# Filter taps in two transfers, two row tiles scaled on GpSimd, the third row tile split, and the first product ahead of the fifth tile

## The chip, the cores and the metric

The kernel runs on one core of a Trainium2 chip. The metric is the device time of one execution in microseconds. Three runs of the kernel before took 942.45, 942.81 and 944.39 us; their median is 942.81.

## The reference

It is one inference step of a two-layer decoder over a prompt of 512 rows and 64 sample rows (8 sequences of 8), each of 1024 features. Layer one is a Conformer convolution layer: h = rms_norm(x) and a, b, z = h @ w_in with w_in of 1024 x 3072. Then a * sigmoid(b) goes through a 31-tap depthwise convolution, and layer norm, silu gates, an output product and a residual follow. Layer two is sparse attention with three branches (compressed, selected, window) over keys and values projected once. What the change touches is the beginning:

```
def rms_norm(x, g):
    xf = x.astype(jnp.float32)
    y = xf * lax.rsqrt(jnp.mean(xf * xf, axis=-1, keepdims=True) + EPS)
    return (y * g.astype(jnp.float32)).astype(x.dtype)
...
    h = rms_norm(x, g_pre)
    a, b, z = jnp.split(h @ w_in, 3, axis=-1)
```

## The kernel before, in words

The 576 rows are five row tiles: four of 128 prompt rows and one (t=4) of the 64 sample rows. Each engine runs one instruction stream in the order written; streams meet only at semaphores. Queues are fed by the engine that issues a transfer: SP (row tiles, weights, state), ScalarE (taps and vectors), GpSimd (page table).

The start works as follows. SP loads the row tiles into `x_first` (L518 to L520), then waits for the third (L559, L560) before it issues weight chunks 0 and 1, two transfers of convolution state after chunk 1 (L563 to L565), and chunks 2 to 5. A weight chunk is a 1024 x 128 piece of w_in (512 KB). Chunk 6 and later ones wait for a slot of a ring of six. ScalarE issues the taps (31 rows into `vec_rows`, L780), six vectors of one row each (L781 to L783), and four small tables.

Per row tile ScalarE squares and sums (L806), VectorE makes the mean (L1272), ScalarE the root (L794), VectorE the reciprocal (L1290, L1292). The scaled tile goes to `xn_a`, which has two slots: VectorE scales tiles 0 to 2 (`first_scale`, L1295), ScalarE tiles 3 and 4 (L811). TensorE transposes a scaled tile in eight 128-column pieces (L1834) into one of two pairs of PSUM banks. VectorE multiplies that by the norm's gain into `h_whole` (`first_turn`, L1300). The gain comes from `vec_rows`, transposed by TensorE after tile 1 (L1839) and copied by VectorE (L1309).

Each product is done as three: a value is split in a high part (fp32r, copied by ScalarE: `first_hi`, `split_hi_a`, both through the copy helper at L777) and a low part (value minus high part: `first_lo` on VectorE, L1284; `split_lo_a` for weights and the low part of tile 3 on GpSimd, L674 and L680). TensorE adds hi x hi, hi x lo and lo x hi.

```
            def first_half(c, hf):
                for k in range(KD):
                    out, here = pb((2, 0)[c] + hf, HT), slice(hf * HT, hf * HT + HT)
                    pe.matmul(out, tile_hi[:, c, k], h_hi[:, k, here], start=(k == 0), stop=False)
                    pe.matmul(out, tile_hi[:, c, k], h_lo[:, k, here], start=False, stop=False)
                    ins = pe.matmul(out, tile_lo[:, c, k], h_hi[:, k, here], start=False, stop=(k == KD - 1))
```

The first two chunks are multiplied in halves of 288 rows: `first_half(0, 0)`, `first_half(1, 0)`, then (0, 1) and (1, 1), each 24 matmuls. The first half needs the tiles 0 and 1 and 32 columns of tile 2, but waits for the low parts of three whole tiles. Chunks 2 to 23 follow as whole products (L1801 to L1803); three chunks feed each of eight convolution blocks on VectorE, ScalarE and GpSimd. `small_tables` on TensorE makes a bias table (L1820) and turns two small rows (L1823), ahead of the transposes of tile 4.

## Time and profile before

| | |
|---|---|
| median of three runs | 942.81 us |
| profiled execution, its own time | 943.98 us |
| its span | 942.2 us |
| TensorE matmul busy | 896.2 us (95%) |
| VectorE, ScalarE, GpSimd busy | 539.6, 439.3, 307.1 us |
| chain that ended last: TensorE's share | 88% |
| granted TensorE clock, mean | 0.989 |

The page gives busy time by engine and the chain of work that ended last. A share of busy time is a mean over stages with different limits, so the start must be read by itself. PE is TensorE, PEld its weight load, DVE VectorE, ACT ScalarE, POOL GpSimd, SP the engine that issues most transfers; a q behind a name is that engine's sequencer issuing a transfer.

### The profile page before, as it was taken

The numbers are of one execution on the slowest core, as the hardware profiler recorded it, in microseconds if no ns is written. First come the engines' busy times: TensorE is split into PE (matmuls) and PEld (weight loads), VectorE is DVE, ScalarE is ACT, GpSimd is POOL, SyncE is SP. The second block draws the span as 40 slices with busy tenths as digits, with TensorE's granted clock in tenths as the row PEclk, the third lists the DMA queues.
The fourth block names the chain that finished last, engine by engine and source line by source line (L and its number), as shares of the span: only waits on it lengthen the run. The fifth ranks groups of instructions, "written<-read, shape, count | busy, mean of one in ns | idle before, by whom it ended". The sixth has DMA issues, their size and how long they took to land.

```text
span 942.2 us, 16720 instructions
## 1 busy us (share of the span) xinstructions
PE 896.2 (95%) x6250; PEld 764.3 (81%) x6250; DVE 539.6 (57%) x1183; ACT 439.3 (47%) x897; POOL 307.1 (33%) x313
## 2 busy tenths in 40 slices
PE   3899999998999999999999999999999999899995
PEld 2799999954478877778989998989999998786653
DVE  2478999998863573331244554555564555544563
ACT  4567677633512533232454555545554555423421
POOL 1479988863370000003014232323233233300000
PEclk9999999998999999999999999999999999999997
DMA  7455433129049443166322231322223002913521
GB/s 205 106 126 167 122 104 88 57 52 304 17 155 371 186 149 90 33 146 181 82 58 49 65 87 29 89 46 68 50 65 67 24 2 53 278 69 109 158 80 35
DMA packets 158137, 99.53 MB, mean 106 GB/s; under 512 B 97173, under 2 KB 146997, under 8 KB 157976
## 3 DMA queue, kind: packets, MB, share of 16 engines
q1 hardware_dynamic: 143198, 79.16, 31.6%
q0 software_dynamic: 4896, 10.32, 3.0%
q10 hardware_dynamic: 9961, 8.97, 2.9%
q8 instruction: 51, 0.84, 0.4%
q14 instruction: 31, 0.25, 0.1%
HBM read 89.58 MB, written 18.85 MB: 115 GB/s over the span
## 4 chain that ended last, share of the span: by engine, by line
PE 88%; ACT 4%; DVE 3%; issue 2%; DMA 1%; POOL 0%; SPq 0%; DVEq 0%; ACTq 0%; POOLq 0%
PE psum L1782 10%; PE psum L2113 7%; PE psum L1881 6%; PE psum L1801 6%; PE psum L1802 6%; PE psum L1803 6%; PE psum L2114 6%; PE psum L2115 6%; PE psum L2208 6%; PE psum L2178 4%; PE psum L2143 4%; PE psum L2161 3%; PE psum L2029 3%; PE psum L2028 3%; PE psum L2030 3%; ACT arena L1188 2%
## 5 line engine op out<-in xcount | busy, mean ns | idle before, releaser
L2113 PE MATMUL psum<-u_hi,tile_hi 128*128 128x288 f32 x464 | 145.9, 314 | 3.3 <-ACT arena L777 3.0
L777 ACT ACTIVATE arena<-psum 128x512 f32<-128x512 f32 (+9 forms) x214 | 82.3, 433 | 142.5 <-PE psum L2030 48.8
L756 POOL TENSOR_SCALAR arena<-arena,kept 128x512 f32<-128x512 f32 (+3 forms) x128 | 83.5, 667 | 174.3 <-DVE kept L1648 174.3
L2114 PE MATMUL psum<-u_lo,tile_hi 128*128 128x288 f32 x464 | 137.4, 296 | 0.0
L2115 PE MATMUL psum<-u_hi,tile_lo 128*128 128x288 f32 x464 | 136.6, 294 | 0.0
L1346 DVE SCALAR_TENSOR_TENSOR psum<-arena,psum 128x512 f32<-128x512 f32 x168 | 127.0, 756 | 6.0
L1801 PE MATMUL psum<-h_hi,tile_hi 128*128 128x288 f32 x352 | 104.2, 296 | 0.0
L1802 PE MATMUL psum<-h_lo,tile_hi 128*128 128x288 f32 x352 | 103.8, 295 | 0.0
L1803 PE MATMUL psum<-h_hi,tile_lo 128*128 128x288 f32 x352 | 103.8, 295 | 0.0
L2113 PEld LDWEIGHTS psum<-u_hi,tile_hi 128*128 128x128 f32 x464 | 87.1, 188 | 14.7 <-issue 6.5
L1579 DVE COPY arena<-psum 128x512 f32<-128x512 f32 (+3 forms) x72 | 37.0, 513 | 101.6 <-PE psum L2161 99.0
L1188 ACT ACTIVATE arena<-arena,kept 128x512 f32<-128x512 f32 (+3 forms) x128 | 70.6, 554 | 44.4 <-DVE kept L1614 44.4
L2114 PEld LDWEIGHTS psum<-u_lo,tile_hi 128*128 128x128 f32 x464 | 87.3, 188 | 1.7 <-issue 1.7
L2115 PEld LDWEIGHTS psum<-u_hi,tile_lo 128*128 128x128 f32 x464 | 87.1, 188 | 0.0
L1782 PE MATMUL psum<-arena 128*128 128x256 f32 (+2 forms) x448 | 84.7, 350 | 0.0
L1782 PEld LDWEIGHTS psum<-arena 128*128 128x128 f32 (+1 forms) x448 | 71.5, 183 | 11.5 <-issue 0.2
L674 POOL TENSOR_TENSOR tile_lo<-tile_whole,tile_hi 128x1024 fp32r<-128x1024 f32 x24 | 59.0, 2464 | 44.8 <-ACT tile_hi L777 44.8
L1802 PEld LDWEIGHTS psum<-h_lo,tile_hi 128*128 128x128 f32 x352 | 66.9, 190 | 0.0
L1801 PEld LDWEIGHTS psum<-h_hi,tile_hi 128*128 128x128 f32 x352 | 66.3, 188 | 0.0
L1803 PEld LDWEIGHTS psum<-h_hi,tile_lo 128*128 128x128 f32 x352 | 66.2, 188 | 0.0
L777 ACT ACTIVATE tile_hi<-tile_whole 128x1024 fp32r<-128x1024 f32 x56 | 59.1, 1056 | 6.7 <-PE psum L1803 5.5
L2208 PE MATMUL psum<-arena 128*128 128x256 f32 x256 | 59.0, 380 | 1.3 <-POOL arena L763 1.3
(295 smaller groups left out, 1835.7 us busy)
## 6 DMA issues: line engine op xcount, KB each, us to landing
tile_whole<-in_b_w_in SPq DMA_DIRECT2D x64, 256.0 KB
tile_whole<-in_a_w_in SPq DMA_DIRECT2D x24, 512.0 KB
arena<-in_cmp_w SPq DMA_DIRECT2D x4, 2048.0 KB, 10.0
kvw_whole<-in_w_kv SPq DMA_DIRECT2D x6, 1024.0 KB, 11.4
bias_copies<-bias_line POOLq DMA_DIRECT2D x4, 1280.0 KB, 23.2
arena<-in_x_prompt SPq DMA_DIRECT2D x8, 512.0 KB, 8.9
arena<-in_a_w_out SPq DMA_DIRECT2D x4, 1024.0 KB, 11.4
arena<-bias_copies SPq DMA_DIRECT2D x16, 256.0 KB, 3.7
```

Of the source, the lines that this page charges most:

```text
L756: pool.tensor_scalar(L, L, rden[:, stat(n) + k:stat(n) + k + 1], gR[:, i, h:h + 1], ALU.mult, ALU.mult).then_inc(S["pn_ready"], 1)
L777: return nc.scalar.activation(out, in_, ACT.Copy, scale=scale)
L1188: nc.scalar.activation(L, L, ACT.Exp, scale=-1.0, bias=mn[:, k:k + 1], accum_out=den[:, k:k + 1]).then_inc(S["exp_done"], 1)
L1346: V.scalar_tensor_tensor(out=acc_p, in0=glu_p[:, m, w:w + SEQ], scalar=tap, in1=acc_p, op0=ALU.mult, op1=ALU.add).then_inc(S["conv_step"], 1)
L1782: ins = pe.matmul(out, l, r, start=(k == 0), stop=(k == len(pairs) - 1))
L1801: pe.matmul(out, w_hi[:, k], h, start=(k == 0), stop=False)
L1802: pe.matmul(out, w_hi[:, k], l, start=False, stop=False)
L1803: ins = pe.matmul(out, w_lo[:, k], h, start=False, stop=(k == KD - 1))
L2113: pe.matmul(pb(7, HT), w_hi, u_hi[:, k, here], start=(k == 0), stop=False)
L2114: pe.matmul(pb(7, HT), w_hi, u_lo[:, k, here], start=False, stop=False)
L2115: ins = pe.matmul(pb(7, HT), w_lo, u_hi[:, k, here], start=False, stop=(k == KD - 1))
L2208: ins = pe.matmul(pb(4 + 2 * (t % 2), 4, CH)[:, c], yT[:, k, t * P:(t + 1) * P], chunk_sb(C_OB + c)[:, k], start=(k == 0), stop=(k == KD - 1))
```

## The change

The taps (31 rows) are loaded by two transfers of 16 and 15 rows. `xn_a` has a place for each tile (tiles 0 and 2 share one, tiles 1 and 4 another). GpSimd scales tiles 3 and 4 (`first_scale_far`) in place of ScalarE. The third tile's turned columns are treated in two parts, 32 and 96 columns, so that there are six row groups (`ROW_GROUPS`) in place of five for `first_turn`, `first_hi` and `first_lo`; the counts of the waits follow. SP no longer waits for the third row tile before the weights. ScalarE does the square of tile 4 after the first three high parts, and the split of weights 0 ahead of the first high part. TensorE transposes the taps after tile 0, and runs `first_half(0, 0)` before the small tables and the transposes of tile 4.

```diff
@@ -136,7 +136,7 @@
...
         last_rows_in = at(R_X + 2 * D, 4, KV, P)
-        xn_a = at(R_C, 2, D)
+        xn_a = [at(R_C, D), at(R_C + D, D), at(R_C, D), at(R_Z + 2560, D), at(R_C + D, D)]
         state_rows = at(R_C + 2 * D, 2, D)
@@ -450,6 +450,8 @@
...
+        ROW_GROUPS = [slice(0, P), slice(P, 2 * P), slice(2 * P, HT), slice(HT, 3 * P), slice(3 * P, 4 * P), slice(4 * P, NT)]
         def square_slot(m):
@@ -556,8 +558,6 @@
...
                     sp.wait_ge(S[name], count)
-                if c == 0:
-                    sp.wait_ge(x_in[2], 16)
                 for src, how in parts:
@@ -674,9 +674,18 @@
...
+            def first_scale_far(t):
+                r = rows(t)
+                pool.wait_ge(S["rs_a"], t - 2)
+                if t == 4:
+                    pool.wait_ge(S["tr_a"], 2)
+                pool.tensor_scalar(xn_a[t][0:r], x_first[0:r, t], rs[0:r, t:t + 1], None, ALU.mult).then_inc(S["xn_a_ready"], 1)
+            first_scale_far(3)
             split_lo_a(0)
+            first_scale_far(4)
             split_lo_a(1)
-            pool.wait_ge(S["hh_ready"], 4)
+            pool.wait_ge(S["hh_ready"], 5)
             pool.tensor_tensor(out=h_lo[:, :, 3 * P:4 * P], in0=h_whole[:, :, 3 * P:4 * P], in1=h_hi[:, :, 3 * P:4 * P],
@@ -777,7 +786,8 @@
...
-            act.dma_start(vec_rows[0:W], I["a_conv_w"][0]).then_inc(S["vec_in"], 16)
+            for lo, hi in ((0, 16), (16, W)):
+                act.dma_start(vec_rows[lo:hi], I["a_conv_w"][0, lo:hi]).then_inc(S["vec_in"], 16)
             for n, name in enumerate(("a_norm_pre", "a_conv_b", "a_ln_g", "a_ln_b", "kv_norm", "b_norm_pre")):
@@ -793,22 +803,21 @@
...
-            def first_hi(t):
-                act.wait_ge(S["h_ready"], t + 1)
-                here = slice(t * P, t * P + rows(t))
+            def first_hi(g):
+                act.wait_ge(S["h_ready"], g + 1)
+                here = ROW_GROUPS[g]
                 copy(h_hi[:, :, here], h_whole[:, :, here]).then_inc(S["hh_ready"], 1)
...
-            for t in range(TT):
+            def first_square(t):
                 r = rows(t)
...
                 first_root(t)
-                if t >= 3:
-                    act.wait_ge(S["rs_a"], t - 2)
-                    act.wait_ge(S["tr_a"], t - 1)
-                    nc.scalar.activation(xn_a[0:r, t % 2], x_first[0:r, t], ACT.Copy, scale=rs[0:r, t:t + 1]).then_inc(S["xn_a_ready"], 1)
+            for t in range(4):
+                first_square(t)
@@ -816,17 +825,19 @@
...
+            split_hi_a(0)
             first_hi(0)
-            split_hi_a(0)
             first_hi(1)
             first_hi(2)
+            first_square(4)
             split_hi_a(1)
+            first_hi(3)
+            first_hi(4)
             act.wait_ge(S["early_mm"], 1)
...
             copy(pe_sb, pb(1, 2, 16)).then_inc(S["line_part"], 1)
-            first_hi(3)
-            first_hi(4)
+            first_hi(5)
             split_hi_a(2)
@@ -1278,9 +1289,9 @@
...
-            def first_lo(t):
-                dve.wait_ge(S["hh_ready"], t + 1)
-                here = slice(t * P, t * P + rows(t))
+            def first_lo(g):
+                dve.wait_ge(S["hh_ready"], g + 1)
+                here = ROW_GROUPS[g]
                 V.tensor_tensor(out=h_lo[:, :, here], in0=h_whole[:, :, here], in1=h_hi[:, :, here], op=ALU.subtract).then_inc(S["hl_ready"], 1)
@@ -1292,12 +1303,14 @@
...
                     dve.wait_ge(S["tr_a"], t - 1)
-                V.tensor_scalar(xn_a[0:r, t % 2], x_first[0:r, t], rs[0:r, t:t + 1], None, ALU.mult).then_inc(S["xn_a_ready"], 1)
-            def first_turn(t):
-                r = rows(t)
+                V.tensor_scalar(xn_a[t][0:r], x_first[0:r, t], rs[0:r, t:t + 1], None, ALU.mult).then_inc(S["xn_a_ready"], 1)
+            def first_turn(g):
+                here = ROW_GROUPS[g]
+                t = here.start // P
+                lo, hi = here.start - t * P, here.stop - t * P
                 dve.wait_ge(S["tr_a"], t + 1)
-                V.tensor_tensor(out=h_whole[:, :, t * P:t * P + r], in0=pb(4 + 2 * (t % 2), KD, P)[:, :, 0:r], in1=gain(0, r),
+                V.tensor_tensor(out=h_whole[:, :, here], in0=pb(4 + 2 * (t % 2), KD, P)[:, :, lo:hi], in1=gain(0, hi - lo),
                                 op=ALU.mult).then_inc(S["h_ready"], 1)
@@ -1307,8 +1320,6 @@
...
             V.tensor_copy(vecT, pb(2, KD, 37)).then_inc(S["vec_ready"], 1)
-            first_mean(4)
-            first_scale(4)
             dve.wait_ge(S["vec_ready"], 1)
@@ -1316,9 +1327,13 @@
...
             first_lo(2)
+            first_mean(4)
+            first_scale(4)
             first_turn(3)
             first_turn(4)
-            first_lo(4)
+            first_lo(3)
+            first_turn(5)
+            first_lo(5)
@@ -1422,7 +1437,7 @@
...
             def kv_rows_lo(t):
-                dve.wait_ge(S["hh_ready"], TT + t + 1)
+                dve.wait_ge(S["hh_ready"], TT + 1 + t + 1)
                 here = slice(t * P, t * P + rows(t))
@@ -1823,21 +1838,22 @@
...
-            for t in range(TT):
+            def turn_a(t):
                 r = rows(t)
-                if t == TT - 1:
-                    small_tables()
                 pe.wait_ge(S["xn_a_ready"], t + 1)
                 if t >= 2:
-                    pe.wait_ge(S["h_ready"], t - 1)
+                    pe.wait_ge(S["h_ready"], (1, 2, 4)[t - 2])
                 for k in range(KD):
-                    ins = pe.transpose(pb(4 + 2 * (t % 2), KD, P)[:, k, 0:r], xn_a[0:r, t % 2, k * P:(k + 1) * P], ident[0:r, 0:r])
+                    ins = pe.transpose(pb(4 + 2 * (t % 2), KD, P)[:, k, 0:r], xn_a[t][0:r, k * P:(k + 1) * P], ident[0:r, 0:r])
                 ins.then_inc(S["tr_a"], 1)
-                if t == 1:
-                    pe.wait_ge(S["vec_in"], 16 * 7)
-                    for k in range(KD):
-                        ins = pe.transpose(pb(2, KD, 37)[:, k], vec_rows[0:37, k * P:(k + 1) * P], ident[0:37, 0:37])
-                    ins.then_inc(S["vec_ps"], 1)
+            turn_a(0)
+            pe.wait_ge(S["vec_in"], 16 * 8)
+            for k in range(KD):
+                ins = pe.transpose(pb(2, KD, 37)[:, k], vec_rows[0:37, k * P:(k + 1) * P], ident[0:37, 0:37])
+            ins.then_inc(S["vec_ps"], 1)
+            for t in range(1, 4):
+                turn_a(t)
@@ -1895,12 +1911,14 @@
...
             first_half(0, 0)
+            small_tables()
+            turn_a(4)
             pe.wait_ge(S["line_part"], 3)
...
             first_half(1, 0)
-            pe.wait_ge(S["hl_ready"], 4)
+            pe.wait_ge(S["hl_ready"], 5)
             pe.wait_ge(S["lo_pool"], 3)
-            pe.wait_ge(S["h_ready"], TT)
+            pe.wait_ge(S["h_ready"], TT + 1)
             for m in range(KD):
@@ -2042,7 +2060,7 @@
...
                 if n < 5:
-                    pe.wait_ge(S["hl_ready"], TT - 1 + (2, 2, 4, 4, 5)[n])
+                    pe.wait_ge(S["hl_ready"], TT + (2, 2, 4, 4, 5)[n])
                 r = rows(t)
```

## Rows read from the trace of the kernel before

**Rows 1.** The page, the chain that ended last, share of the span by engine.
```profile
PE 88%; ACT 4%; DVE 3%; issue 2%; DMA 1%; POOL 0%; SPq 0%; DVEq 0%; ACTq 0%; POOLq 0%
```

**Rows 2.** Stretches: length, busy PE PEld DVE ACT POOL (count), clock, DMA, GB/s.
```profile
0.00:10.00 10.00, 0.49 (x3) 0.53 (x4) 1.07 (x3) 2.84 (x5) 2.48 (x14) 1.00 0.77 243
50.00:100.00 50.00, 50.00 (x381) 50.00 (x381) 42.45 (x62) 32.00 (x41) 42.49 (x28) 1.00 0.55 150
220.00:240.00 20.00, 15.86 (x49) 8.52 (x49) 16.28 (x21) 10.71 (x17) 5.85 (x3) 0.74 0.65 216
```

**Rows 3.** The chain in order of time, 0 to 80 us: start, length, what.
```profile
2.16 13.26 DMA arena<-in_x_prompt
```

**Rows 4.** Single microseconds of the start; the last two columns are DMA share, GB/s.
```profile
7.00:8.00 1.00, 0.00 (x0) 0.00 (x0) 0.02 (x1) 0.95 (x2) 0.00 (x0) 1.00 1.07 362
11.00:12.00 1.00, 0.45 (x3) 0.04 (x1) 0.10 (x1) 0.87 (x2) 0.00 (x0) 1.00 0.06 25
16.00:17.00 1.00, 0.56 (x6) 0.57 (x6) 0.15 (x1) 0.78 (x3) 0.00 (x0) 1.00 1.11 319
```

**Rows 5.** Timeline of ScalarE: start, length, line, out<-in, count, idle before and releaser.
```profile
6.80 1.06 ACT L806 ACTIVATE arena<-arena 128x1024 f32<-128x1024 f32 x1 [2.10 <-DMA arena<-in_x_prompt]
...
8.17 0.20 ACT L794 ACTIVATE kept<-kept 128x1 f32<-128x1 f32 x1 [0.22 <-DVE kept L1272]
10.72 1.06 ACT L806 ACTIVATE arena<-arena 128x1024 f32<-128x1024 f32 x1 [2.35 <-DMA arena<-in_x_prompt]
...
13.39 1.06 ACT L806 ACTIVATE arena<-arena 128x1024 f32<-128x1024 f32 x1 [1.10 <-DMA arena<-in_x_prompt]
...
15.44 1.06 ACT L806 ACTIVATE arena<-arena 128x1024 f32<-128x1024 f32 x1 [0.48 <-DMA arena<-in_x_prompt]
...
25.37 1.04 ACT L777 ACTIVATE tile_hi<-tile_whole 128x1024 fp32r<-128x1024 f32 x1
...
29.80 0.57 ACT L777 ACTIVATE arena<-psum 16x512 f32<-16x512 f32 x1
```

**Rows 6.** Timeline of VectorE.
```profile
8.61 0.75 DVE L1295 TENSOR_SCALAR arena<-arena,kept 128x1024 f32<-128x1024 f32 x1
...
19.96 2.36 DVE L1300 TENSOR_TENSOR h_whole<-psum,arena 128x1024 f32<-128x1024 f32 x2
25.50 1.23 DVE L1284 TENSOR_TENSOR h_lo<-h_whole,h_hi 128x1024 fp32r<-128x1024 f32 x1 [3.18 <-ACT h_hi L777]
...
27.77 3.39 DVE L1284 TENSOR_TENSOR h_lo<-h_whole,h_hi 128x1024 fp32r<-128x1024 f32 x2
```

**Rows 7.** Timeline of TensorE.
```profile
9.51 1.94 PE L1834 MATMUL psum<-kept,arena 128*128 128x128 f32 x8 [9.51 <-DVE arena L1295]
...
16.43 1.07 PE L1839 MATMUL psum<-kept,arena 37*128 37x37 f32 x8 [1.13 <-DMA arena<-in_b_norm_pre]
...
24.91 1.89 PE L1820 MATMUL psum<-arena 32*16 32x512 f32 x2
26.73 0.39 PE L1823 MATMUL psum<-kept,arena 16*128 16x16 f32 x2
28.00 1.09 PE L1834 MATMUL psum<-kept,arena 64*128 64x64 f32 x8 [0.89 <-DVE h_whole L1300]
31.27 0.58 PE L1889 MATMUL psum<-h_hi,tile_hi 128*128 128x288 f32 x1 [2.17 <-DVE h_lo L1284]
...
36.66 0.29 PE L1890 MATMUL psum<-h_lo,tile_hi 128*128 128x288 f32 x1
```

**Rows 8.** GpSimd: its timeline, then one of its groups by shape (count | busy, mean ns).
```profile
26.50 2.45 POOL L674 TENSOR_TENSOR tile_lo<-tile_whole,tile_hi 128x1024 fp32r<-128x1024 f32 x1 [22.98 <-ACT tile_hi L777]
29.97 3.44 POOL L674 TENSOR_TENSOR tile_lo<-tile_whole,tile_hi 128x1024 fp32r<-128x1024 f32 x1 [1.03 <-ACT tile_hi L777]
...
L756 POOL TENSOR_SCALAR arena<-arena,kept 128x512 f32<-128x512 f32 x32 | 24.4, 774 | 102.1 <-DVE kept L1648 102.1
```

**Rows 9.** Timeline of SP's queue.
```profile
0.75 1.83 SPq L520 DMA_DIRECT2D arena<-in_x_prompt  x4
```

## The prediction

> **What bounds the kernel now.** I read three views in this order. The page's chain that ended last is 88% TensorE by share of the span [rows 1]. The table of stretches shows TensorE busy 50.00 of 50.00 us in a projection stretch, and only 15.86 of 20.00 us around 220 to 240 us, at a granted clock of 0.74 [rows 2]. The reader should see that once the projections run TensorE has no holes, so nearly every microsecond by which its stream starts earlier is a microsecond off the end. The chain in order of time then shows what the start waits for: 13.26 us of the prompt's fourth row tile (t=3) in flight, before its normalisation can begin [rows 3]. The first dense product starts at 31.27 [rows 7]. The case is therefore the first 31 us.
>
> **Why the rows come so late.** The table by microsecond [rows 4] shows the DMA engines at share 1.07 and 362 GB/s in 7 to 8 us, but at 0.06 and 25 GB/s in 11 to 12 us. A share of 0.06 is 1/16: one engine works alone. In the first 10 us 243 GB/s moved 2.4 MB, about the five row tiles (2.3 MB): the rest of the wait is for one engine's share. One transfer of this stretch has a row count that sixteen engines can't share evenly: the taps, 31 rows of 4 KB, 124 KB. On one engine at 25 GB/s they take 124/25 = 5.0 us, which is the length of the tail (10 to 15 us). The squares of the four prompt tiles start at 6.80, 10.72, 13.39 and 15.44 [rows 5]: 2 to 4 us apart, where 512 KB at 362 GB/s is 1.4 us. SP issues all row tiles from 0.75 us on [rows 9], and its next issue waits for the third tile, so the weights' bytes only show at 16 to 17 us (319 GB/s) [rows 4].
>
> **The change part by part.**
>
> *Taps in two transfers (16 and 15 rows).* If they spread over 16 and 15 engines, the busiest engine carries 8 KB of taps in place of 124. The tiles then follow each other at 1.4 us. With the first at 6.1 us (6.80, less the 0.7 by which halved sharing with the taps may bring it forward; bounds 5.4 and 6.8), they land at about 6.1, 7.5, 8.9 and 10.3, the fifth at 11. Bounds: if both parts stay on one engine, the arrivals are those of now. If only the 15 rows do, they cost 60/25 = 2.4 us. I take the even spread. The vectors' seven rows are seen by TensorE at 16.43 now, last behind that same engine [rows 7]. They should be there by 8, and are first needed at 10.7.
> The Trainium skill, "DMA: Bandwidth & Descriptors", section "Why a DMA increments its semaphore by 16 and not by 1", says that a transfer uses the largest number of engines up to 16 that divides its slowest dimension: 1 engine for 31 rows, 15 for 15 rows. The trace agrees for the first. For the second no row here shows it.
>
> *SP's wait on the third tile gone.* Chunks 0 and 1, the state rows and chunks 2 to 5 queue straight behind the row tiles. All eight transfers move forward, about 4 MB. If the queue serves in order, chunk 0 (512 KB at 319 GB/s = 1.6 us from about 10, and 1 to 1.5 us until it is seen, an estimate from the tail, whose 5.0 us end at 15 while the last vector is seen at 16.43) is there at 12.5 to 13.2 instead of after 16. Cost to the tiles: nothing if in order, up to the whole backlog if not (second-last rival).
>
> *ScalarE.* One tile takes 6.80 to 8.37 (square, VectorE's mean, root ending 8.17 + 0.20) [rows 5], 1.6 us. Four in a row from 6.1 start at 6.1, 7.7, 9.3, 10.9: now the engine sets the pace, not the DMA. VectorE's reciprocal of the fourth ends about 1.8 us after its square starts, 12.7. The fifth tile's square and both scalings (copies at L811) leave this stretch. The copy of weights 0 (1.04) [rows 5] runs at 13.2 to 14.3 and then the first h_hi at 14.5 to 15.6.
>
> *GpSimd's two scalings.* No row shows a 128x1024 scaling there. The nearest is 0.77 us for 128x512 [rows 8]; below, 0.75 us as VectorE's [rows 6], above twice 0.77 = 1.55. I take 1.2. The fourth tile is scaled by 13.9, needed at 16.5; the fifth by 21.3, needed at 26. Both are hidden, with 2.6 us and 4.7 us of cover; the first one holds the split of weights 0 back by 1.2 us at most.
>
> *TensorE.* Row tile 0: 8.8 to 10.8 (as at 9.51, 1.94 us). Taps: to 11.8 (1.07). [rows 7] Row tile 1: to 13.8. VectorE's copy of the taps follows its fourth reciprocal, 12.7 to 13.2, then the turns 0 and 1 (2.36 for both [rows 6]): 13.25 to 14.4 and to 15.6. Row tile 2 waits for turn 0: 14.6 to 16.5; row tile 3: to 18.5.
>
> *VectorE up to the first product.* Here two-input work of VectorE meets GpSimd's. Alone, a low part takes 1.23 us; the pair at 27.77 takes 3.39 instead of 2.4 [rows 6], beside the split of weights 0 that ends at 28.95 (26.50 + 2.45), and the split after it takes 3.44 instead of 2.45 [rows 8]. Each waited for the other's end. So the low part of tile 0, ready at 15.6, waits for the split of weights 0 (13.9 or 14.3 to 16.4 or 16.7) and ends at 17.6. Turn of the 32-column part 0.35, low part 1: 1.15, low part of the 32 columns 0.35: 19.5. Before, the third tile's whole turn and low part stood here (1.22 + 1.15), now a quarter: the split in two parts is worth 1.7 us. The first product starts at about 19.5 in place of 31.27: 11.8 us earlier.
> The Trainium skill, "SBUF — State Buffer", section "SBUF: two separate sides", calls the port pair shared by VectorE and GpSimd an exclusive lock held for a whole instruction. It speaks against putting more on GpSimd here. By it the low part of tile 0 loses the 0.8 to 1.1 us above; had they only shared bandwidth it would lose about half. The trace's pair agrees with the lock.
>
> *What moves in behind the first half product.* Now the small tables (1.89 and 0.39) and the fifth tile's transposes (1.09) stand ahead of the first product [rows 7]. They go between its first and second piece, in the stream that sets the end. The first half product is 24 products: 22 of them at 0.24 us (288 columns: the 1.2 GHz level, though the granted-clock column reads 1.00) from 31.27, then from 36.66 on 0.13 (2.4 GHz) [rows 7], as in the 381 products of 50.00 us [rows 2]; TensorE had run dense products for 5.2 us before it rose; the transposes and tables before them had not raised it. New: 19.5 to 25.2 at the lower level. Before the second piece come the tables, 1.9 + 0.4 at the lower level, about 1.0 + 0.2 at the upper, tile 4's transposes, 1.1 or 0.6, and ScalarE's copy of the tables (0.57 [rows 5]), beside tile 4. I take 2.4 with the wait for the copy: 27.6. The second piece, 24 x 0.13 = 3.2: 30.8. Now the same point is 36.92 + 3.2 = 40.1. Beside it: the fifth tile's scaling ends at 21.3, the turns 3 and 4 at 22.1, the two low parts at 24.6 and (GpSimd) 27, turn 5 at 27.8, its low part at 29.2: all ahead of 30.8. Cover is 1.6 us for the last; if it is late, that is the next wait.
>
> *Sum.* 40.1 - 30.8 = 9.3 us. Put otherwise: 11.8 earlier, 2.5 given back by tables and tile 4. Waits added on TensorE (taps before tile 1, the fifth tile in the middle) have their releasers done by 8 and 21.3. The profiled execution took 943.98 (span 942.2); the runs' median is 942.81, 1.2 lower. A difference of 9.3 taken off the median gives **933.5 us**. Behind 31 us everything waits on TensorE's progress (weights, taps, compression), so it shifts as a block.
>
> **Rivals.**
> - *The tail is not the taps* (or both parts stay on one engine). Tiles land as now, 15.44 for the fourth. The taps, then ahead of tile 1 on TensorE, arrive at 16.4 and hold tile 1 to 17.5 to 19.5; low parts end near 24, the first product starts at 24 rather than 19.5. Gain 4.8: 938.0. For: the trace does not name the engine. Against: 124 KB at 25 GB/s fits the tail.
> - *The clock does not rise in the first half product*, being broken off after 5.7 us by the light tables (which at 24.91 now did not raise it). The tables stay at 2.3 and tile 4 at 1.1, and up to 22 further products cost 0.11 more: 1.1 + 2.4 = 3.5, gain 5.8: 937.0. Against: it rose after 5.2 us now. In the other direction a rise within the first piece gives up to 1 us.
> - *A later stage gives it back.* At 220 to 240 TensorE idles and the clock is 0.74; how long it stays low may fall otherwise by 1 to 3 us either way. The stretch prices it: 20 us at 0.74 is 5.2 us of clock [rows 2]. Gain 6 to 12.
> - *The weights hold back the row tiles* (the one on the slow side). If the queue's transfers share the engines instead of following each other, the 4 MB issued from 3.2 us on compete with tiles 2 and 3. Each 512 KB ahead of the fourth tile costs 1.6 us; past 9.3/1.6, about six of them (3 MB), the change loses. All eight ahead: the tile lands at 10.3 + 12.8 = 23.1 and the first turn starts at 25.5. From there 6.25 us (13.25 to 19.5 above) and 11.3 (19.5 to 30.8) bring the third piece to 43.0, 2.9 later than now: 945.7. Against: the five row tiles, issued within 2.5 us, landed one after another.
>
> **Chances.** Forecast 68%, with its own range 931 to 936. Taps not the tail 9%. Clock not rising 10%. A later stage taking 3 us or more 6%. Weights ahead of tiles 5% (of which 4 end slower). 2% for no effect by several small ones. A difference of 0.2% (1.9 us) is about what a measurement can tell. Faster 0.93, same 0.03, slower 0.04. Range 930.5 to 938.0: it takes in the first two rivals and the later rise or fall of the clock.
>
> **What would show it.** In the profile of after: the DMA share between 10 and 15 us at about 1 and no stretch at 0.06; squares 1.6 us apart; GpSimd scaling near 1.2; first dense product at 19 to 20.5; spacing 0.13 from about 25; the start of the third piece near 30.8; and in 50 to 200 us the same pattern 9 us earlier. It is wrong if the tail stays, if the first row tile is later than 7, if low part 5 or the table copy holds TensorE by over 1 us, or if the fourth square starts after 12.

## The result, and the profile after

| | before | after |
|---|---|---|
| median of the runs | 943.39 us (n 5) | 936.62 us (n 5: 933.32, 934.04, 936.62, 937.53, 937.62) |
| ratio, 95% interval | | 0.9933 (0.991 to 0.9956) |
| profiled execution, span | 943.98, 942.2 us | 933.32, 931.4 us |

The change makes the kernel faster by 6.3 us (0.9933 of 943.39; interval 4.2 to 8.5), where 9.3 were forecast (933.5 us; measured 936.62). The same kernel measured again (run a_again): ratio 0.9922 (0.9902 to 0.9943), 7.3 us. The profiled execution of after is the fastest of its five. Its distance to the profile of before (10.7 us) is therefore not the gain, and has to be taken apart by stage.

The page of after, the chain that ended last: it answers to [rows 1].
```profile
PE 89%; DVE 4%; ACT 3%; issue 2%; DMA 1%; POOL 0%; SPq 0%; DVEq 0%; ACTq 0%; POOLq 0%
```
Stretches of after, columns as in [rows 2, 4]:
```profile
7.00:8.00 1.00, 0.00 (x0) 0.00 (x0) 0.64 (x3) 0.78 (x3) 0.00 (x0) 1.00 1.01 402
9.00:10.00 1.00, 1.00 (x7) 1.00 (x6) 0.88 (x3) 0.95 (x2) 0.00 (x0) 1.00 1.17 199
11.00:12.00 1.00, 1.00 (x8) 0.93 (x8) 0.38 (x1) 0.32 (x1) 0.00 (x0) 1.00 1.22 156
12.00:13.00 1.00, 1.00 (x7) 1.00 (x5) 0.14 (x1) 0.83 (x2) 0.00 (x0) 1.00 1.19 292
50.00:100.00 50.00, 50.00 (x379) 50.00 (x378) 42.35 (x61) 33.53 (x43) 45.15 (x29) 1.00 0.56 156
220.00:240.00 20.00, 17.39 (x50) 8.60 (x51) 17.87 (x24) 8.22 (x12) 6.80 (x3) 1.00 0.33 114
```
The tail is gone: the share of the DMA engines in 11 to 12 us is 1.22 where it was 0.06 [rows 4]. But in 9 to 12 us the engines are busy and move only 156 to 199 GB/s. The projections are as full as before. The stretch at 220 to 240 us has a granted clock of 1.00, where it was 0.74 [rows 2]; at 212 to 232 us, where the same work now lies, it is 1.00 too.

ScalarE of after, the four squares and the split of weights 0, against [rows 5]:
```profile
5.87 1.06 ACT L816 ACTIVATE arena<-arena 128x1024 f32<-128x1024 f32 x1 [0.44 <-issue]
...
7.35 1.04 ACT L816 ACTIVATE arena<-arena 128x1024 f32<-128x1024 f32 x1
...
8.81 1.04 ACT L816 ACTIVATE arena<-arena 128x1024 f32<-128x1024 f32 x1
...
11.68 1.06 ACT L816 ACTIVATE arena<-arena 128x1024 f32<-128x1024 f32 x1 [1.31 <-DMA arena<-in_x_prompt]
...
14.48 1.06 ACT L786 ACTIVATE tile_hi<-tile_whole 128x1024 fp32r<-128x1024 f32 x1 [1.23 <-DMA tile_whole<-in_a_w_in]
```
Three squares follow each other at the engine's own pace (1.47 us). The fourth still waits for its row tile, and the split waits for chunk 0.

GpSimd of after, then VectorE of after (its first half product is released by the first row, its third piece by the last):
```profile
13.55 2.84 POOL L682 TENSOR_SCALAR arena<-arena,kept 128x1024 f32<-128x1024 f32 x1 [10.06 <-DVE kept L1301]
16.38 2.35 POOL L674 TENSOR_TENSOR tile_lo<-tile_whole,tile_hi 128x1024 fp32r<-128x1024 f32 x1
22.34 2.83 POOL L682 TENSOR_SCALAR arena<-arena,kept 64x1024 f32<-64x1024 f32 x1 [3.61 <-DVE kept L1301]
25.15 2.35 POOL L674 TENSOR_TENSOR tile_lo<-tile_whole,tile_hi 128x1024 fp32r<-128x1024 f32 x1
27.47 2.37 POOL L689 TENSOR_TENSOR h_lo<-h_whole,h_hi 128x1024 fp32r<-128x1024 f32 x1
```
```profile
16.51 3.30 DVE L1295 TENSOR_TENSOR h_lo<-h_whole,h_hi 128x1024 fp32r<-128x1024 f32 x1 [0.31 <-ACT h_hi L786]
...
24.15 6.50 DVE L1295 TENSOR_TENSOR h_lo<-h_whole,h_hi 128x768 fp32r<-128x768 f32 x1
30.57 0.68 DVE L1313 TENSOR_TENSOR h_whole<-psum,arena 128x512 f32<-128x512 f32 x1
31.95 0.69 DVE L1295 TENSOR_TENSOR h_lo<-h_whole,h_hi 128x512 fp32r<-128x512 f32 x1 [0.70 <-ACT h_hi L786]
```
A scaling takes 2.84 us for 128 rows and 2.83 for 64. The low part of row group 3 takes 6.50 us for 0.94 us of work and ends 0.8 us behind the last of GpSimd's three instructions (27.47 + 2.37 = 29.84; 24.15 + 6.50 = 30.65).

TensorE of after, against [rows 7]:
```profile
10.45 1.07 PE L1853 MATMUL psum<-kept,arena 37*128 37x37 f32 x8
...
21.71 0.58 PE L1905 MATMUL psum<-h_hi,tile_hi 128*128 128x288 f32 x1 [3.08 <-DVE h_lo L1295]
...
24.97 0.36 PE L1906 MATMUL psum<-h_lo,tile_hi 128*128 128x288 f32 x1
...
26.57 1.03 PE L1835 MATMUL psum<-arena 32*16 32x512 f32 x2
27.53 0.29 PE L1838 MATMUL psum<-kept,arena 16*128 16x16 f32 x2
27.75 0.71 PE L1847 MATMUL psum<-kept,arena 64*128 64x64 f32 x8
28.39 0.40 PE L1905 MATMUL psum<-h_hi,tile_hi 128*128 128x288 f32 x1
...
32.70 0.40 PE L1905 MATMUL psum<-h_hi,tile_hi 128*128 128x288 f32 x1 [0.87 <-DVE h_lo L1295]
```
The first product starts at 21.71 (31.27 before), the third piece at 32.70 (40.1): 7.4 us, and the last row shows a wait that was not there before. At 232.00 against 224.31, where the compression's products start behind the last state transposes, it is 7.7. The 22 products there take 12.35 us before and 9.37 after, which makes 10.7. First before, then after:
```profile
232.00 12.35 PE L1881 MATMUL psum<-arena 128*128 128x495 f32 x22 [1.16 <-issue]
```
```profile
224.31 9.37 PE L1897 MATMUL psum<-arena 128*128 128x495 f32 x22 [1.16 <-issue]
```
So 7.4 to 7.7 us come from the start, and the other 3.0 from the clock of one later stretch.

### The profile page after: what moved, and what is told of

Its sections match the earlier page's. It is cut to its first block, busy times and chain, and to the rows that moved or that the text cites. A ratio compares the mean times of both kernels' runs of the same rounds, so it can differ in the third digit from the quotient of the medians.

```text
span 931.4 us, 16723 instructions
## 1 busy us (share of the span) xinstructions
PE 890.2 (96%) x6250; PEld 761.1 (82%) x6250; DVE 544.3 (58%) x1185; ACT 437.0 (47%) x896; POOL 310.4 (33%) x315
## 4 chain that ended last, share of the span: by engine, by line
PE 89%; DVE 4%; ACT 3%; issue 2%; DMA 1%; POOL 0%; SPq 0%; DVEq 0%; ACTq 0%; POOLq 0%
PE psum L1797 10%; PE psum L2131 7%; PE psum L2132 6%; PE psum L2133 6%; PE psum L1816 6%; PE psum L1817 6%; PE psum L1818 6%; PE psum L1897 6%; PE psum L2226 6%; PE psum L2196 4%; PE psum L2161 4%; PE psum L2179 3%; PE psum L2047 3%; PE psum L2046 3%; PE psum L2048 3%
```

## The experiments

The runs are in three groups, each on one chip, with runs of the kernel before on the same chip: a_again, taps_one, sp_wait and scale_act (median of before 941.6), before_taps, fill_mid, pool_order and pool_forms (942.79), and the last three (942.01). "Third piece" is its start on TensorE, the point up to which the change works. Differences in us between two kernels are given only within a group; they are of the means, with a 95% interval. Between groups only the ratios to before can be compared.

**a_again**: the changed kernel, unaltered.

> The changed kernel, unaltered. The executions of it so far fall in two groups, 933.3 and 934.0, and 936.6 to 937.6, at mean granted clocks of 0.994 and 0.992 against 0.989. Theory C: the 3 us between the groups are one stretch at half clock around the transposes of the compression rows (10 us at 0.50 in the profile before, none in the profile after), so the next executions fall in the same two groups, and a profile of one at 0.989 shows a stretch at 0.50 near 219 to 230 us and the 22 products after it in about 12.4 instead of 9.4 us. Rival: the spread lies in the first 35 us (another arrival of tiles or weights); then the profiles differ there and not at 220.

Measured 933.92 (n 6), ratio 0.9922 (0.9902 to 0.9943). The fourth square starts at 11.00 (after 11.68), the first product at 21.04, the third piece at 32.02; the start moves by 0.7 us with the arrival of the rows and chunk 0. The 22 products, of the same code in the same place:
```profile
223.22 11.06 PE L1897 MATMUL psum<-arena 128*128 128x495 f32 x22 [1.16 <-issue]
```
That is 11.06, between 9.37 and before's 12.35. In the profiles of the other kernels it is 9.37, 11.06, 11.57 or 11.61. What falls or rises here is not set by the kernel's code alone, and one profile cannot credit it to the change. The two groups of the expectation came again: 936.72 at a mean clock of 0.989, the other five 932.98 to 934.80 at 0.992 to 0.996. The profiled execution is one of the five, so where the 3 us of the other group lie was not seen.

**taps_one**: the changed kernel, taps in one transfer again.
```
-            for lo, hi in ((0, 16), (16, W)):
-                act.dma_start(vec_rows[lo:hi], I["a_conv_w"][0, lo:hi])...
+            act.dma_start(vec_rows[0:W], I["a_conv_w"][0]).then_inc(S["vec_in"], 16)
...
-            pe.wait_ge(S["vec_in"], 16 * 8)
+            pe.wait_ge(S["vec_in"], 16 * 7)
```


> The changed kernel with the 31 rows of taps in one transfer again. Theory A (the taps sit on one DMA engine and make it the last for every row tile): the squares start near 6.8, 10.7, 13.4 and 15.4 again, the taps are transposed at 16.4 or later, the first product starts at 24 to 26 instead of 21.7, and the time is 3 to 5 us above the changed kernel's (for the same clock), 938 to 941. Rival B (the tail came from the wait of SP or from elsewhere): squares about 1.5 us apart as now, time unchanged.

Measured 939.76 (n 10), ratio 0.9974 (0.9959 to 0.9989): 4.9 us slower than a_again (3.5 to 6.4). Its stretch 13 to 14 us, then its second and fourth square:
```profile
13.00:14.00 1.00, 0.00 (x0) 0.00 (x0) 0.74 (x2) 0.19 (x1) 0.00 (x0) 1.00 0.06 25
```
```profile
11.62 1.06 ACT L815 ACTIVATE arena<-arena 128x1024 f32<-128x1024 f32 x1 [2.95 <-DMA arena<-in_x_prompt]
...
16.45 1.06 ACT L815 ACTIVATE arena<-arena 128x1024 f32<-128x1024 f32 x1 [0.49 <-DMA arena<-in_x_prompt]
```
The tail at 0.06 and 25 GB/s is back, and all row tiles are late with it. The first product starts at 26.49, the third piece at 37.47. The 31-row transfer is the tail; with it two thirds of the gain are gone. The 2.4 us that are left (1.0 to 3.9, from the ratio) are what the rest of the change brings while the tail stays.

**before_taps**: the kernel before with only this edit (the inverse of the diff above).

> The kernel before with only the taps in two transfers (16 and 15 rows). Theory A (the 31-row transfer is the last on one DMA engine, all row tiles wait for it): the squares start at about 5.9, 7.4, 8.9 and 10.5 to 11.7, the taps are turned by 12.5, SP's wait ends near 8.5 so the weights come early as well, and the first product starts 4 to 5 us earlier, at 26 to 27.5; time 4 to 5.5 us below the kernel before. Theory G (the gain needs the reordering too: ScalarE's and VectorE's old order takes up the early rows): 0 to 2 us.

Measured 936.62 (n 4), ratio 0.9936 (0.9913 to 0.9959), 6.0 us. Its first and fourth square, and its first product:
```profile
5.78 1.06 ACT L807 ACTIVATE arena<-arena 128x1024 f32<-128x1024 f32 x1 [0.35 <-issue]
...
10.92 1.06 ACT L807 ACTIVATE arena<-arena 128x1024 f32<-128x1024 f32 x1 [0.64 <-DMA arena<-in_x_prompt]
```
```profile
26.73 0.58 PE L1890 MATMUL psum<-h_hi,tile_hi 128*128 128x288 f32 x1 [2.57 <-DVE h_lo L1285]
```
The third piece starts at 35.03: 5.1 us earlier than before. All the reordering together brings it 2.3 to 3.0 further (32.70, 32.02). Of the 6.0 us up to 0.9 may be the later clock (its 22 products take 9.37). In the whole kernel's time the intervals of before_taps and the changed kernel overlap, so with split taps that rest is shown by the trace alone; with one transfer the time shows it too (2.4 us, taps_one).

**sp_wait**: the changed kernel with SP's wait on the third tile put back.
```
                 for name, count in frees(c):
                     sp.wait_ge(S[name], count)
+                if c == 0:
+                    sp.wait_ge(x_in[2], 16)
```


> The changed kernel with SP's wait on the third row tile back. Theory A: the weights in flight early cost the row tiles little; the fourth tile, seen at 11.68 now, is seen at 10.3 to 11.7, and chunk 0, seen at 14.48 now, comes at 13 to 15, since the third tile lands by 9 and the wait then holds for little: time within 1 us of the changed kernel. Rival D (the weights compete with the fourth row tile): the fourth square starts at 10.3, the chunk does not come later, and the kernel is up to 1.4 us faster than the changed one. Rival E (the early weights are what brought the gain): chunk 0 comes at 16 or later and the kernel is 2 us or more slower.

Measured 933.72 (n 4), ratio 0.9922 (0.9894 to 0.995), 0.4 us below a_again (between 2.7 below and 2.0 above). SP's queue in it:
```profile
8.50 1.02 SPq L564 DMA_DIRECT2D tile_whole<-in_a_w_in  x2
9.56 2.72 SPq L567 DMA_DIRECT2D arena<-in_state_conv  x2
```
The weights are issued at 8.50 instead of 3.4. The fourth square starts at 11.10 (a_again 11.00), the copy of chunk 0 at 13.84 (13.73), the first product at 21.13 (21.04). Issuing 5 us earlier brings nothing and harms nothing: without the wait SP is busy 3.9 us with issuing the first two chunks and 4.7 with the state rows (a_again), with it 1.0 and 2.7. So issuing them at 3.4 does not hold back the row tiles. Both kernels issue them before the fourth tile is there, though, so what the first chunk costs that tile is not tested.

**scale_act**: the changed kernel, both scalings on ScalarE as before.
```
-            first_scale_far(3)
...
-            first_scale_far(4)
...
+                if t >= 3:
...
+                    nc.scalar.activation(xn_a[t][0:r], x_first[0:r, t], ACT.Copy, scale=rs[0:r, t:t + 1]).then_inc(S["xn_a_ready"], 1)
```


> The changed kernel with the tiles 3 and 4 scaled on ScalarE (1.15 us each) instead of GpSimd (2.84 us each). Theory A (the GpSimd scaling of 2.84 us holds back the split of weights 0 and by the shared access the low part of tile 0, 3.30 us; the second one lets the low part of row group 3 take 6.50 us): the split of weights 0 starts at 15.6, the low part of tile 0 ends near 19.1 instead of 19.8, the first product starts at 20.9 to 21.2 instead of 21.7, the third piece no longer waits 0.9 us, and starts 1 to 2 us earlier, at 31 to 31.7. Time 1 to 2 us below the changed kernel's for the same clock. Rival F (ScalarE becomes the bound, its first copies 1.15 us later): the first product is not earlier, time the same or 1 us slower.

Measured 931.85 (n 4), ratio 0.9891 (0.9867 to 0.9915), 2.3 us below a_again (0.3 to 4.3). ScalarE in it, then VectorE:
```profile
13.77 1.15 ACT L820 ACTIVATE arena<-arena,kept 128x1024 f32<-128x1024 f32 x1 [0.23 <-DVE kept L1304]
```
```profile
16.85 2.55 DVE L1298 TENSOR_TENSOR h_lo<-h_whole,h_hi 128x1024 fp32r<-128x1024 f32 x1 [0.36 <-ACT h_hi L784]
...
24.73 2.50 DVE L1298 TENSOR_TENSOR h_lo<-h_whole,h_hi 128x768 fp32r<-128x768 f32 x1 [0.91 <-ACT h_hi L784]
```
The scaling costs 1.15 us there, the low part of group 3 2.50 instead of 6.50, and the third piece starts at 31.28 without a wait, although the fourth row tile was 1 us later than in a_again (11.97). The first product starts at 21.30, 9.33 us behind the fourth square; in after and a_again it is 10.03 and 10.04. The move to GpSimd is the part of the change that costs time. How much is less sure: the trace shows 0.7 us at the first product and 1.0 behind it, and the spans of the two profiles are equal (932.0 and 932.1; the 22 products take 11.57 here, and this profile is of the slowest of the four executions).

**pool_forms**: on GpSimd, the fourth tile scaled with a second operation by 1.0 (same values), the fifth in two single-operation halves of 512 columns.
```
+                if t == 3:
+                    pool.tensor_scalar(xn_a[t][0:r], x_first[0:r, t], rs[0:r, t:t + 1], 1.0, ALU.mult, ALU.mult)...
+                else:
+                    pool.tensor_scalar(xn_a[t][0:r, 0:512], x_first[0:r, t, 0:512], rs[0:r, t:t + 1], None, ALU.mult)
...
```


> The changed kernel with tile 3 scaled on GpSimd in the form with a second multiplication by 1.0, and tile 4 in two instructions of 512 columns. If 2.84 us is the price per element (2.8 ns a column) the first takes 2.8 and the two together 2.8. If the form with one operation is the slow one, the first takes about 1.6 to 1.9 and the pair stays at 2.8. If it is the length (1024 columns) that costs, the pair takes 1.5.

One execution, 937.24 (a granted clock of 0.91 in 880 to 900 us, where after has 1.00). GpSimd:
```profile
13.80 1.11 POOL L683 TENSOR_SCALAR arena<-arena,kept 128x1024 f32<-128x1024 f32 x1 [10.28 <-DVE kept L1305]
...
21.69 1.56 POOL L685 TENSOR_SCALAR arena<-arena,kept 64x512 f32<-64x512 f32 x1 [3.61 <-DVE kept L1305]
```
The same 1024 columns take 1.11 us with two operations (1.6 to 1.9 were expected) and 2.84 with one; 512 columns with one take 1.56, about half of it. So it is not a price of long instructions or of many rows: it is the form with one operation. One profile of one execution shows it here, and the four scalings with two operations in forms_order and forms_order_fill confirm it (1.11 to 1.12, for 128 and for 64 rows).
VectorE's low part of group 3 in the same profile, and the split of weights 1 on GpSimd:
```profile
23.49 2.12 DVE L1299 TENSOR_TENSOR h_lo<-h_whole,h_hi 128x768 fp32r<-128x768 f32 x1
```
```profile
24.77 3.06 POOL L674 TENSOR_TENSOR tile_lo<-tile_whole,tile_hi 128x1024 fp32r<-128x1024 f32 x1
```
Here the split stood ready behind the scaling as well, and the low part took 2.12 us, not 6.50: it ends 0.82 behind the second half of the scaling (24.79), and the split takes 3.06 in place of 2.35. So VectorE does not always lose to the next instruction.
The Trainium skill, "GPSIMD Engine Reference", section "3.1 Elementwise — side-by-side cycle accounting", gives 1.03 cycles per element for up to two operations. For 1024 columns at its 1.2 GHz that is an estimate of 0.88 us: the form with two operations comes near it (1.11), the form with one does not (2.84).

**pool_order**: the changed kernel, the split of weights 1 on GpSimd kept behind VectorE's low part of group 3.
```
             first_scale_far(4)
+            pool.wait_ge(S["hl_ready"], 4)
             split_lo_a(1)
```


> The changed kernel with GpSimd's split of weights 1 held until the low part of row group 3 is done on VectorE. Theory A (VectorE's low part of 96 columns takes 6.50 us because three GpSimd instructions in a row take the shared access, 25.2 to 29.8): it now ends at 26.2 (1 to 2.1 us after its start), turn 5 follows tile 4's transposes at 28.5, the third piece waits for nothing but the low parts on GpSimd (end near 30.9), and starts 1.0 to 1.2 us earlier. Time 0.9 to 1.2 us lower. Rival I: the split of weights 1, 1 us later, holds back the second piece (28.39 now) and takes the gain.

Measured 933.29 (n 4), ratio 0.991 (0.9881 to 0.9938). VectorE, then GpSimd:
```profile
24.43 0.94 DVE L1296 TENSOR_TENSOR h_lo<-h_whole,h_hi 128x768 fp32r<-128x768 f32 x1
```
```profile
22.63 2.83 POOL L682 TENSOR_SCALAR arena<-arena,kept 64x1024 f32<-64x1024 f32 x1 [3.62 <-DVE kept L1302]
25.46 2.37 POOL L674 TENSOR_TENSOR tile_lo<-tile_whole,tile_hi 128x1024 fp32r<-128x1024 f32 x1
```
The low part took 0.94 us, and it ran beside the slow scaling. In after it began at the same point of that scaling (1.8 us into it) and took 6.50; there the next GpSimd instruction stood ready behind the scaling, here it did not. The third piece starts 9.98 us after the first product instead of 10.99 in after, without a wait, and the first pieces are equally long (4.87 and 4.86). The total time does not show this 1.0 us: the interval of the ratio overlaps that of a_again.

**tables_first**: the changed kernel, small tables and fifth tile's transposes ahead of the first product again.
```
             turn_a(3)
+            small_tables()
+            turn_a(4)
...
-                    small_tables()
-                    turn_a(4)
```


> The changed kernel with the small tables and the fifth tile's transposes ahead of the first product again, as before the change; all else as changed. Theory J (moving the product ahead of them is worth what the wait for the fifth tile costs): the fifth tile is scaled at about 25.2, its transposes end near 26.3 and only then the first product starts (21.7 now); with the clock low again for some 5 us the third piece starts at 33.5 to 35, 1 to 2.5 us later, and the time is 1 to 2.5 us above the changed kernel's. Rival K (tables and tile 4 cost the same in front as behind): within 0.7 us of it.

Measured 935.92 (n 4), ratio 0.9928 (0.99 to 0.9956). TensorE:
```profile
24.00 1.11 PE L1847 MATMUL psum<-kept,arena 64*128 64x64 f32 x8 [3.64 <-POOL arena L682]
25.04 0.61 PE L1907 MATMUL psum<-h_hi,tile_hi 128*128 128x288 f32 x1
```
The transposes wait 3.64 us for the scaling and the first product starts at 25.04, the third piece at 33.67: 1.0 to 1.7 us later than in after and a_again. That is what the move is worth at that point, while the scaling takes 2.83 us; with the faster one the wait would be shorter. The ratio's interval overlaps that of a_again, and the profile also has a clock of 0.91 in 880 to 900, so its total says little.

**fill_mid**: the changed kernel, four 128x128 products of the identity with itself (result unused) after each of the last six groups of transposes ahead of the compression's products.
```
+                if 1 < b:
+                    for _ in range(4):
+                        pe.matmul(pb(7, P), ident, ident, start=True, stop=True)
```


> The changed kernel with four more small matmuls (identity times identity into an unused PSUM bank) after each of the last six groups of compression transposes, where TensorE idles some 0.5 to 1.2 us a time. Theory C (the spread of 3 us is a fall of the clock to half in this stretch, at a moment that shifts from run to run): the 22 products after it take 9.4 us in the profile, no 0.50 there, the slow group of times is gone, and the median is 0.5 to 2 us below the changed kernel's. Rival H: the clock falls all the same, and the filling adds up to 1 us to the chain of transposes.

Measured 935.22 (n 6), ratio 0.9915 (0.9896 to 0.9933). The 22 products take 9.37 us, but they start at 225.56, 13.3 us behind the projections' end at 212.24; in a_again it is 11.7 (211.54 to 223.22). The fillers took 1.6 us, as much as the clock gives here against a_again (11.06 to 9.37): too many of them. The expected 0.5 to 2 us did not come, and since five profiles without fillers in this place have 9.37 as well, this one does not show that they held the clock.

**forms_order**: the changed kernel with both cures for GpSimd: two-operation scaling, and pool_order's wait.
```
-                pool.tensor_scalar(xn_a[t][0:r], x_first[0:r, t], rs[0:r, t:t + 1], None, ALU.mult)...
+                pool.tensor_scalar(xn_a[t][0:r], x_first[0:r, t], rs[0:r, t:t + 1], 1.0, ALU.mult, ALU.mult)...
...
+            pool.wait_ge(S["hl_ready"], 4)
```


> The changed kernel with both GpSimd scalings in the form with a second multiplication by 1.0 (1.11 us in the profile of the forms, 2.84 with one operation), and the split of weights 1 held until the low part of row group 3 is done. Theory A: the split of weights 0 starts at 15.6, the first product at 20.9 to 21.1, no wait before the third piece, which starts at 31 to 31.5: 1.2 to 1.7 us earlier than in the changed kernel, time 1.2 to 1.7 us lower, below both kernels. Rival L (the last word is tile arrival and the clock's rise, which comes at the same time whatever the start): the first product starts 0.7 us earlier and the third piece only 0.7 us.

Measured 932.99 (n 6), ratio 0.9902 (0.9878 to 0.9926). Its first product starts at 20.24 and its third piece at 30.21: 1.8 us earlier than in a_again, 0.8 of it at the first product (0.1 of that is the fourth tile's earlier arrival), 1.0 behind it. The intervals of the two ratios overlap. TensorE is still not at the upper clock throughout:
```profile
20.00:24.00 4.00, 3.76 (x18) 3.79 (x19) 3.29 (x6) 3.22 (x6) 1.42 (x2) 0.62 1.15 290
```

**forms_order_fill**: the same, with few fillers in TensorE's idle times: three ahead of the third row tile's transposes, four behind the fourth's, one per group of the later transposes (none in the first, four in the last).
```
+                if t == 2:
+                    for _ in range(3):
+                        pe.matmul(pb(3, P), ident, ident, start=True, stop=True)
...
+            for _ in range(4):
+                pe.matmul(pb(3, P), ident, ident, start=True, stop=True)
...
+                for _ in range(0 if b < 1 else 4 if b == DB - 1 else 1):
+                    pe.matmul(pb(7, P), ident, ident, start=True, stop=True)
```


> The same, with small matmuls of identity by identity into unused PSUM banks: three before the third tile's transposes, four behind the fourth's, where TensorE idles about 2 us each, and one after each group of compression transposes but the first, with four after the last. Theory M (the clock is low in the first 4 to 5 us of products because TensorE had idled before them, and falls in the second place for the same reason): the first products run at 0.13 us apart from the start or within 2 us of it, the third piece starts another 1 to 2.5 us earlier, and the 22 products later take 9.4 us; 1.5 to 4 us below the kernel without filling. Rival N (the clock rises and falls as before, filling only delays): same or up to 1.5 us slower.

Measured 930.22 (n 6), ratio 0.988 (0.9858 to 0.9902), 2.1 us below forms_order (0.2 to 4.1). It is the lowest ratio of all, though scale_act's interval overlaps it. The stretches that had the lower clock:
```profile
20.00:24.00 4.00, 3.69 (x25) 3.31 (x26) 3.36 (x6) 3.30 (x6) 1.34 (x2) 1.00 1.16 288
24.00:28.00 4.00, 3.29 (x25) 2.54 (x24) 1.72 (x2) 2.37 (x5) 4.00 (x2) 1.00 0.56 142
220.00:240.00 20.00, 19.73 (x51) 9.19 (x50) 18.64 (x28) 9.52 (x13) 6.79 (x3) 1.00 0.21 72
```
Two rows of TensorE: the next wait, and the third piece's first product.
```profile
26.25 0.37 PE L1911 MATMUL psum<-h_hi,tile_hi 128*128 128x288 f32 x1 [0.71 <-POOL tile_lo L674]
...
29.51 0.29 PE L1911 MATMUL psum<-h_hi,tile_hi 128*128 128x288 f32 x1
```
All 24 products of the first half product run at 0.13 us (3.3 us in place of 4.9), and the second piece now waits 0.71 us for the split of weights 1, so 0.7 us are left of the 1.5. In none of the twelve other profiles do all 24 run at 0.13: the first piece takes 4.86 to 5.9 us there. The rest of the distance of the two spans (929.9 and 927.3) is mostly the 22 products, 9.37 for 11.06, and 9.37 comes without fillers too.

Starts of the third piece and spans, beside the one clock of the middle: before 40.1 and 942.2 (22 products 12.35); before_taps 35.03 and 933.4 (9.37); after 32.70 and 931.4 (9.37); a_again 32.02 and 932.1 (11.06); forms_order 30.21 and 929.9 (11.06); forms_order_fill 29.51 and 927.3 (9.37). Span less third piece less 22 products is 888.6 to 889.8 in five of these and 888.4 in the last, which has fillers in the middle. In the other kernels it is 888.6 to 889.4, but 891.7 and 892.2 in pool_forms and tables_first, which have the clock of 0.91 in 880 to 900, and 891.6 in fill_mid, of which its fillers are 1.6. Behind the start everything does shift as a block, but for the clock.

## Why the prediction was right, and where it was off

The mechanism held: the 31-row transfer was the tail, and what the start gained came off the end. The time lies in the stated range, but a third of the forecast gain did not come: 9.3 us is outside the interval of 4.2 to 8.5. Of the missing 3.0 us 1.9 lie in the start, which gained 7.4 and not 9.3; the other 1.1 is within what the executions differ by. Of the signs that the prediction named, the tail, the squares and the clock of the first piece came; the scaling near 1.2, the first product at 19 to 20.5 and the third piece near 30.8 did not.

The prediction's own steps, in time:

| step | forecast | after | a_again |
|---|---|---|---|
| squares | 6.1, 7.7, 9.3, 10.9 | 5.87, 7.35, 8.81, 11.68 | ..., 11.00 |
| copy of chunk 0 starts | 13.2 | 14.48 | 13.73 |
| GpSimd's scaling | 1.2 (0.75 to 1.55) | 2.84 | 2.84 |
| low part of tile 0 ends | 17.6 | 19.81 | 19.14 |
| first product | 19.5 | 21.71 | 21.04 |
| first piece | 5.7 | 4.86 | 5.57 |
| tables, tile 4, wait | 2.4 | 1.82 | 1.83 |
| second piece, with the wait behind it | 3.2 | 4.31 | 3.58 |
| third piece | 30.8 | 32.70 | 32.02 |

*The tail.* Right. It is the 31-row transfer: taken back alone it costs 4.9 us, made alone it brings 6.0. The trace's record of landings shows the one engine as well. A row tile arrives in 16 parts; of the fourth tile before, 15 parts are in by 10.28 us and the last at 15.42, and its square starts at 15.44. In after no microsecond at share 0.06 is left, and three squares run 1.5 us apart. Both parts of the taps spread: the seven transfers of taps and vectors before leave two updates each on their semaphore, 14 in all; the eight of after leave 44, which is 12 for the six vectors and 32 for the two parts. Had the 15 rows gone to one engine, it would be 30.

*The scaling on GpSimd: the term that was mis-sized.* I took 1.2 us from a 128x512 row of 0.77 [rows 8], with 1.55 as the upper bound; it takes 2.84. L756 multiplies by two columns in one instruction, the new scaling by one with no second operation: the row was of another form, and the bound doubled it without asking what else differed than the length. pool_forms shows that the form makes the difference: 2.84 with one operation, 1.11 with two. The step "holds the split of weights 0 back by 1.2 us at most" did hold in its number: the split could start at 15.54 and did at 16.38, 0.85 us late. The first product got most of that delay: it starts 10.0 us behind the fourth square with the slow scaling (after, a_again, sp_wait, pool_order, fill_mid) and 9.3 behind it with either cure (scale_act, forms_order). Of the 1.5 us by which a_again's first product is late, with its fourth square nearly on time, this is 0.7, and the later chunk 0 is 0.5.

*"All ahead of 30.8".* This failed. The low parts 3 and 4 were put at 24.6 and 27, the last low part at 29.2 with 1.6 us of cover. It starts at 31.95, and the third piece waits 0.87 us. The prediction named that as the next wait. What it missed is that VectorE's low part can lose to several GpSimd instructions in a row (6.48 to 6.51 us in six profiles, but 2.12 in pool_forms): the fifth tile's scaling, the split of weights 1 and the low part of tile 3. One added wait on GpSimd (pool_order) brings it back from 6.50 to 0.94 us.
The Trainium skill, "SBUF — State Buffer", section "SBUF: two separate sides", lets whichever instruction starts first hold the shared pair of ports to its end. The 3.30 us of the first low part agree (1.08 us behind the end of the split). The low part that ran in 0.94 us inside a 2.83 us scaling (pool_order) does not, nor does one that started inside that scaling, ahead of the split, and lost to it (6.50, after). There the measurement decides.

*Rows and chunk 0.* The fourth square starts at 10.9 to 12.0 in all kernels with the split taps, for 10.9 in the forecast, and by then it waits for its tile, which was to land at 10.3. Chunk 0 is 0.4 to 1.5 us behind the forecast. The queue was priced at 319 to 362 GB/s throughout; in 9 to 12 us it moved 156 to 199 in after. before_taps has it as well (196 and 175 in 9 to 11 us), with the weights' first issue at 8.3, so their issue at 3.4 is not the cause. In a_again 15 of the fourth tile's 16 parts are in by 9.75 and the last at 10.98, so one part is late again, by about 1 us; the six vectors of one row land one behind another from 7.09 to 9.85. Whether both sit on the same engine the trace does not name, and in after five parts are late. The cause stays open.

*SP's wait gone.* It was taken as what brings chunk 0 forward; sp_wait shows it is worth nothing that can be measured, since with the split taps the third tile is there by 8.5.

*The third tile in two parts.* The 1.9 us between the low part of tile 0 and the first product came as forecast (19.81 to 21.71), but no run takes the split of the tile back alone, nor the new order on ScalarE. What each is worth is argued from the rows.

*The clock.* It rose within the first piece, after 3.3 us of products (24.97 less 21.71) where it had taken 5.2 before; in a_again it was 4.9. The forecast gave this up to 1 us; the pieces got shorter by 0.8 and, with the tables at the upper clock, 0.6. But the early rise did not bring the third piece forward. It starts 10.96 to 10.99 us behind the first product in after, a_again, sp_wait, fill_mid and taps_one, whose first pieces take 4.86 to 5.9 us: the low parts set it there, and a faster first piece only waits longer. It would pay only with that wait gone. The errors of the sum are +2.2 (first product), -0.8 (first piece), -0.6 (tables) and +1.1 (second piece with its wait): 1.9 us, the distance from 30.8 to 32.70.

*The later stretch.* The rival of 1 to 3 us either way was right in size and wrong in being tied to the change. With the same code in that place the 22 products take 9.37, 11.06, 11.57 or 11.61 us in one or another profile (12.35 before), and a second stretch, in 880 to 900, shows 0.91 in two kernels. It makes up 3.0 of the 10.7 us by which the two profiles differ there. Whether the change makes a low clock there rarer can't be told from single profiles.

*The other rivals.* "The tail is not the taps" fell by taps_one and before_taps, "the clock does not rise" by 24.97. "The weights hold back the row tiles" fell in the size that would make the kernel slower: with all eight transfers ahead the tile lands at 23.1, and the fourth square starts at 11.68.

## What to carry over

Look for a stretch in which the DMA engines' share falls to that of one engine, and for the transfer that fits its length: at the start of this kernel 124 KB in 31 rows delayed the last of 2 MB of other rows by 4.5 us (15.44 to 10.92), and cutting it in 16 and 15 rows undid that. Price an instruction only by a row of the same form, and before work is moved to an engine that shares an access with another, list what it then does in one unbroken run, for that is how long the other may wait. A gain at the start is best read at the last instruction that the change touches; the total of one profile carries the clock of other stretches too.

## What the runs showed of the hardware that was not expected

- GpSimd's fp32 scaling by a column takes 2.84 us for 1024 columns with one operation, 1.11 with a second one (by 1.0), and about the same for 64 rows as for 128 (2.83 and 2.84).
- A VectorE low part of 128x768 that starts 1.8 us into such a scaling takes 0.94 us when nothing stands ready behind the scaling on GpSimd (pool_order), and 6.48 to 6.51 us, in six profiles, when the next instruction does. One that starts 0.25 us into the second half of a scaling in two halves takes 2.12 with the next instruction ready (pool_forms). How the access is handed on was not tried further, and starts and lengths on GpSimd are rough in the records.
- With seven small products in two idle times of TensorE ahead of the first product, its 24 products ran at 0.13 us from the first on, at a granted clock of 1.00 in 20 to 24 us where it was 0.62 in forms_order. The spacing is what counts: the column reads 1.00 in that stretch of a_again too, where the products are 0.24 apart. For the ten in the middle (220 to 240 us, 1.00 for 0.91) this is not shown, as 1.00 comes there without them too.
- A row tile is complete only with the last of its 16 parts: of the third tile before, 15 parts are in by 7.90 us and the last at 13.37; after the split of the taps all 16 are in by 8.58.
- The granted clock is 0.91 in 880 to 900 us of tables_first and pool_forms and 1.00 in after: a low stretch can come and go near the end as in the middle. The 0.50 in 913 to 919 of after is not one of these: before has 0.51 in 924 to 930, where the same work lies.
